# Where a rarely taken branch stands in a mixture-of-experts stage, and a PSUM bank for the last sums

## The reference, cut to what matters

```python
for g in range(N_GROUPS):
    a = jnp.einsum('td,edf->tef', t, w_gate[g])
    b = jnp.einsum('td,edf->tef', t, w_up[g])
    hid = jax.nn.silu(a) * b * comb[:, g, :, None]
    y = y + jnp.einsum('tef,efd->td', hid, w_down[g])
```

## Time and profile before

| | us |
|---|---|
| median of three runs | 1003.07 |
| the runs | 1004.33, 1001.78, 1003.07 |
| the profiled execution | 1001.91 |
| its span | 999.9 |
| TensorE busy | 946.3 (95%) |
| VectorE busy | 498.5 (50%) |
| ScalarE busy | 329.4 (33%) |

### The profile page before, as it was taken

How to read it: one execution, slowest core, us unless ns; L and a number is a source line. 1 busy time by engine, 2 the same in 40 slices (tenths; PEclk the granted TensorE clock), 3 DMA queues, 4 the chain that set the end, 5 groups by cost and what they waited for, 6 DMA issues and landing times.

```text
span 999.9 us, 14232 instructions
## 1 busy us (share of the span) xinstructions
PE 946.3 (95%) x5926; PEld 670.9 (67%) x5926; DVE 498.5 (50%) x868; ACT 329.4 (33%) x525; POOL 36.4 (4%) x39
## 2 busy tenths in 40 slices
PE   5999999999999999999898899999988899999997
PEld 5997734444444444344443689878988799999885
DVE  6694613222222222232221686988977657667642
ACT  5723210000000010000000656555464645554531
POOL 1000000000000000000000000232210000000000
PEclk9999999999999999999998999999999999999998
DMA  9946999999999999999999943623242424555301
GB/s 358 406 188 263 420 408 425 425 431 430 430 430 431 430 431 429 433 429 430 431 423 416 387 164 105 233 85 147 107 169 86 168 106 169 179 194 209 137 1 42
DMA packets 27797, 289.45 MB, mean 289 GB/s; under 512 B 3024, under 2 KB 5328, under 8 KB 11088
## 3 DMA queue, kind: packets, MB, share of 16 engines
q1 hardware_dynamic: 27008, 286.91, 70.4%
q10 hardware_dynamic: 720, 1.57, 0.4%
HBM read 287.43 MB, written 1.05 MB: 288 GB/s over the span
## 4 chain that ended last, share of the span: by engine, by line
PE 77%; DMA 9%; DVE 8%; ACT 4%; issue 2%; SPq 0%; DVEq 0%; ACTq 0%
PE ps L279 77%; DMA ring<-in_moe 8%; DVE wl L275 3%; ACT wh L268 2%; DVE arena L1497 1%; DMA vec<-in_vec 1%; PE ps L1011 1%; DVE arena L564 0%; ACT arena L1796 0%; ACT in_h L634 0%; DVE arena L1703 0%; DVE arena L1839 0%; ACT arena L1799 0%; DVE arena L365 0%; PE ps L1983 0%
## 5 line engine op out<-in xcount | busy, mean ns | idle before, releaser
L279 PE MATMUL ps<-ring,arena 128*64 128x512 f32 x1216 | 340.6, 597 | 10.2 <-issue 9.6
L279 PEld LDWEIGHTS ps<-ring,arena 128*64 128x64 f32 x1216 | 109.8, 137 | 170.0 <-issue 167.8
L275 DVE TENSOR_TENSOR wl<-ring,wh 128x1024 fp32r<-128x1024 f32 x150 | 180.7, 1234 | 58.6 <-ACT wh L268 58.6
L279 PE MATMUL ps<-arena 128*64 128x512 f32 (+3 forms) x416 | 162.9, 542 | 0.8 <-DVE arena L559 0.5
L268 ACT ACTIVATE wh<-ring 128x1024 fp32r<-128x1024 f32 x150 | 151.5, 1050 | 32.3 <-PE ps L279 28.2
L1116 DVE SCALAR_TENSOR_TENSOR arena<-ps,arena 128x512 f32<-128x512 f32 x16 | 12.0, 751 | 209.1 <-PE ps L279 209.1
L279 PE MATMUL ps<-up_h,wh 128*128 128x256 f32 x352 | 88.3, 286 | 4.6 <-DVE up_l L1920 4.6
L279 PE MATMUL ps<-up_l,wh 128*128 128x256 f32 x352 | 87.8, 284 | 0.0
L279 PEld LDWEIGHTS ps<-arena 128*64 128x64 f32 (+1 forms) x416 | 53.4, 142 | 47.0 <-issue 41.2
L1186 ACT ACTIVATE y_h<-ps 128x512 fp32r<-128x512 f32 x32 | 19.1, 597 | 158.4 <-PE ps L279 158.4
L279 PEld LDWEIGHTS ps<-up_h,wh 128*128 128x128 f32 x352 | 67.5, 192 | 5.0 <-issue 4.9
(11 more groups left out here) (262 smaller groups left out, 1505.1 us busy)
## 6 DMA issues: line engine op xcount, KB each, us to landing
ring<-in_moe SPq DMA_DIRECT2D x69, 2048.0 KB, 24.3
arena<-in_moe SPq DMA_DIRECT2D x17, 2048.0 KB, 25.5
ring<-in_w_in SPq DMA_DIRECT2D x12, 2048.0 KB, 9.4
ring<-in_w_up SPq DMA_DIRECT2D x11, 2048.0 KB, 7.9
ring<-in_moe SPq DMA_DIRECT2D x20, 512.0 KB, 15.4
ring<-in_w_dn SPq DMA_DIRECT2D x5, 2048.0 KB, 8.0
ring<-in_w_out SPq DMA_DIRECT2D x4, 2048.0 KB, 15.4
arena<-in_moe SPq DMA_DIRECT2D x12, 512.0 KB, 15.0
```

The costliest lines, as they stand in the source:

```text
L275: e.tensor_tensor(wl(i), raw_piece(i), wh(i), SUB).then_inc(*lo.up(i))
L279: return e.matmul(o, l, r, start=first, stop=final, skip_group_check=True)
```

## The change

Two edits. First, the `If` (`over`) moves from ahead of pair 15 to ahead of pair 14, on all three engines. Pair 15's place weights (`weigh(15)` on TensorE, `weighed(15)` on VectorE), which were made in pair 14, move with it, to a place just in front of it; the waits at the top of `over_dve`, which run only where the body runs, name the pair before. Second, in pair 15 the scatter of quarter 3 goes to bank 4 in place of bank 7, without the wait for the add of quarter 0.

```diff
--- before.py
+++ after.py
@@ -903,7 +903,10 @@
         scat = sig("scat", [(q, z) for q in range(NP) for z in range(4)])
         acc = sig("acc", [(q, z) for q in range(NP) for z in range(4)])
         part = sig("part", [("g", 1), ("g", 3), ("g", 5), ("u", 3)])
-        ZB = [7, 5, 6, 7]
+
+        def zb(q, z):
+
+            return 4 if (q, z) == (NP - 1, 3) else (7, 5, 6, 7)[z]
 
         def parted(q, n):
 
@@ -962,7 +965,7 @@
                     k = mm(e, ps[3][64 * r:64 * r + 64, 0:256], ident[0:NE, x:x + 1].to_broadcast([NE, CAP]), POT[0:NE, :], True,
                            True)
                 k.then_inc(*spread.up(q))
-                if q + 1 < NP:
+                if q + 1 < NP - 1:
                     if q % 2:
                         e.wait_ge(*picked.at((q + 1) // 2))
                     weigh(q + 1)
@@ -1046,12 +1049,12 @@
                 for z in (2 * n, 2 * n + 1):
                     if z == 0 and q:
                         e.wait_ge(*acc.at(q - 1, 3))
-                    if z == 3:
+                    if z == 3 and q < NP - 1:
                         e.wait_ge(*acc.at(q, 0))
                     for y in range(2):
                         f = (2 * z + y) * 128 - 512 * n
-                        mm(e, ps[ZB[z]][:, y * 256:y * 256 + 256], h[:, f:f + 128], SCT[:, :], True, False)
-                        k = mm(e, ps[ZB[z]][:, y * 256:y * 256 + 256], l[:, f:f + 128], SCT[:, :], False, True)
+                        mm(e, ps[zb(q, z)][:, y * 256:y * 256 + 256], h[:, f:f + 128], SCT[:, :], True, False)
+                        k = mm(e, ps[zb(q, z)][:, y * 256:y * 256 + 256], l[:, f:f + 128], SCT[:, :], False, True)
                     k.then_inc(*scat.up(q, z))
 
             gather(0)
@@ -1059,7 +1062,8 @@
             for q in range(NP):
                 if q == 1:
                     v = many(e)
-                elif q == NP - 1:
+                elif q == NP - 2:
+                    weigh(NP - 1)
                     over(e, v, over_pe)
                 half(q, "g")
                 if q == 0:
@@ -1127,7 +1131,7 @@
                     e.wait_ge(*scat.at(q, z))
                     if q:
                         e.wait_ge(*acc.at(q - 1, z))
-                    e.tensor_tensor(x, x, ps[ZB[z]][:, :], ADD).then_inc(*acc.up(q, z))
+                    e.tensor_tensor(x, x, ps[zb(q, z)][:, :], ADD).then_inc(*acc.up(q, z))
 
             e.wait_ge(*slots.at(0))
             pick(0)
@@ -1139,13 +1143,14 @@
             for q in range(NP):
                 if q == 1:
                     v = many(e)
-                elif q == NP - 1:
+                elif q == NP - 2:
+                    weighed(NP - 1)
                     over(e, v, over_dve)
                 hidden(q)
                 if q:
                     add(q - 1, 1)
                 placed(q)
-                if q + 1 < NP:
+                if q + 1 < NP - 1:
                     weighed(q + 1)
                 if q % 2 == 0 and q + 2 < NP:
                     pick(q // 2 + 1)
@@ -1252,8 +1257,8 @@
                     k.then_inc(*ov_d.up(x, j))
 
         def over_dve(e):
-            e.wait_ge(*ctr.at(NP - 2))
-            e.wait_ge(*acc.at(NP - 2, 1))
+            e.wait_ge(*ctr.at(NP - 3))
+            e.wait_ge(*acc.at(NP - 3, 1))
             e.wait_ge(*ppm.at(3))
             e.tensor_tensor(X1F, X1H[:, :, :], X1L[:, :, :], ADD).then_inc(*ov_in.up("sum"))
             e.wait_ge(*ov_in.at("sum"))
```

## The result

The change makes the kernel slower: 1007.13 us (median of 5 runs, 1005.48 to 1009.84) against 1003.07 (5 runs, 1001.55 to 1004.67), ratio 1.0040, 95% interval 1.0026 to 1.0053. The profiled execution took 1009.84 us, the longest of the five, with a span of 1007.9.

The account below looks back on a forecast made before the run. Weights were taken to set the pace up to 519.8 us, TensorE behind it, ScalarE the last 4 us. Part 1 at -0.1 us plus part 2 at 0 gave a median of 1003.0 us, range 999.6 to 1005.6.

Parts of the forecast that it names:

- The jump, 3.20 us: At pair 14's head: the moved check's jump costs the 3.20 us it cost ahead of pair 15.
- the jump is dearer where it is now: Rival, at pair 14's head: a second fetch or closer engine jumps add up to 3.2 us, 1006.2; chance 0.04.
- The clock: Behind the moved jump: TensorE's idleness lowers the granted clock in pair 14's gate half, costing 2.87 us.
- the 2.66 us left it high: Pair 13's idle stretch ahead of 480.56: 2.66 us of idleness did not lower TensorE's clock.
- slower: the idle stretch ahead of the gate product: Rival, 560.2 to 562.4: 2.2 us of unbroken idleness lowers the clock, +2.87 us, 1005.8; chance 0.12.
- No slack: Behind the new place: only 0.29 us of transfer wait is left to absorb the stall.
- Part 2, nothing: Pair 15's last scatter quarter in its own bank: gain 0, at most 1.25 us, since nobody is late for it.
- The other engines' jumps and the weights' new place, nothing: At pair 14: VectorE's and ScalarE's jumps add no TensorE wait; the place weights cost 0.55 us there, as before.

Follow-up runs that it names:

- move_only: Kernel before with only the check moved ahead of pair 14, pair 15's place weights in front; last quarter still in bank 7: 1006.15 us.
- weigh_late: Kernel before with pair 15's place weights moved directly in front of the check, which stays ahead of pair 15: 1004.78 us.
- weigh_early: Changed kernel with pair 15's place weights ahead of pair 13's down product, so the moved jump follows a scatter: 1003.51 us.
- bank_only: Kernel before with only the last quarter of pair 15 sent to bank 4; check stays ahead of pair 15: 1003.28 us.
- after_short: Changed kernel with the check's body cut to one expert in place of 32: 1004.73 us.
- outline_14: Changed kernel with the check's body out of line on TensorE, which falls through; ScalarE and VectorE keep their jumps: 997.77 us.
- weigh_then_fill: Changed kernel with 8 idle matmuls between the place weights and the moved jump: 1008.44 us, one run.
- after_small: Changed kernel with pair 14's up and down weights sent in quarters of their columns, so in smaller packets: 1006.58 us.
- outline_15: Kernel before with the check's body out of line on TensorE, which falls through at pair 15; other engines keep their jumps: 997.53 us.
- fill_jump: Kernel before with 20 idle matmuls directly in front of the jump ahead of pair 15: 1005.66 us.
- over_13: Kernel before with the check ahead of pair 13, the rest unmoved: 1001.83 us.

## Why the prediction was wrong

The forecast was 1003.0 us in a range of 999.6 to 1005.6; the median is 1007.13.

- **The step that failed: "The jump, 3.20 us ... I take the row, since the queue of weights is as full as it was there."** Weights and jump together took 511.79 - 506.58 = 5.21 us in place of 0.55 + 3.20 = 3.75, and 5.1 to 5.2 in move_only and weigh_late too. What raises the price is not the queue of weights, nor in the main the pair (3.62 us of idleness in weigh_early at pair 14, 3.14 in the kernel before at pair 15), but the small matmuls that the change puts directly in front of the jump. I priced weights and jump each from a row in which the other wasn't next to it, and added them. With 5.21 in the sum the forecast would have been 1004.5, inside the range. The rest of the miss, some 2.7 us, goes with the clock as far as is known: the next two points. The rival "the jump is dearer where it is now" was right in kind; it had 0.04, and a wrong cause.
- **The clock.** I took one figure, 2.87 us, for one drop. In the place where I put it, behind the moved jump, it cost 2.6 (the two halves take 16.58 us, and 13.96 at the full clock), so that term was about right, though with the whole body it varies from 1.3 (move_only, bank_only) to 2.9 (before). What the sum lacks is two other places where the clock drops in some executions and not in others. One is pair 13's wait of 2.7 us: the clock is low behind it in five profiles (after, move_only, after_short, outline_14, weigh_then_fill), and high in nine. My "the 2.66 us left it high" was one draw of it. All five have the check ahead of pair 14 (outline_14 on ScalarE and VectorE alone), as have only two of the nine (after_small, weigh_early). That is more than chance would easily give, yet nothing that the change touches runs before this wait; I have no mechanism for it, and one profile per kernel doesn't show one.
- **The rival "slower: the idle stretch ahead of the gate product" came true in the profile and was not the edit's doing.** It is the other of the two places. Without matmuls to fill the stretch, seven of eight profiles with bank 4 have the drop, and four of nine with bank 7 (move_only, outline_15, fill_jump, over_13), where the idleness is in two pieces of 1.25 and 0.73 us. So 2.2 us without a break aren't needed for it. It may come more often with the one long stretch, but bank_only's median moved by 0.2 us. Its price was 1.5 us in the product, against the 2.87 I gave it.
- **No slack: right.** No transfer was waited for behind the new place. The down product began 1.49 us after the turn, where I had 1.29, and pair 15's head came 8.16 us after that, where I had 8.15.
- **Part 2, nothing: right,** by bank_only, 0.9999 (0.9988 to 1.0009). The last four scatter groups run without a break and TensorE idles 2.26 us (2.2 forecast).
- **The other engines' jumps and the weights' new place, nothing: right,** by outline_14 against outline_15.

What remains: the profiles give 2.7 us for the weights in front of the jump; move_only's median is 3.1 us over before and the changed kernel's 4.1, with an interval of 2.6 to 5.3. The gap goes with the clock: the changed kernel's five executions have a mean granted clock of 0.985 to 0.987, move_only's twelve 0.986 to 0.989, and at 0.987 the two take the same (1005.48 and 1005.64 us; five of 1005.22 to 1006.91). In which stretch it was low in executions without a profile, and why it is low more often in the changed kernel, is not shown.

The Trainium skill's rule in "Runtime: NRT & Kernel Launch", section "Instruction fetch mechanics", that a taken branch to a target which isn't loaded waits for a fetch, holds here: with the same computation and no branch taken on TensorE before the end of its work, 5.5 and 9.4 us are gone (outline_15, outline_14). The 108 ns of "Advanced Engine Details and Errata", section "Control Flow Timing", are no price for such a branch: 3.0 to 5.3 us of idleness were measured with the whole body, in one piece or in two.

## What to carry to other kernels

A rarely taken branch over a large body costs its fetch on the path that falls to the side of the jump, so lay the body out of line and let the common case fall through: that was worth about 5 us here, and moving the branch was worth nothing. If it must be jumped over, look at what stands directly in front of it, and don't add the prices of two neighbours read from rows where they weren't neighbours. A matrix engine that waits some 2 us on its critical path may pay again behind the wait through its clock, in some executions; work that nobody reads, put into two such waits, took 3.8 us off.

## What the runs showed of the hardware that I had not expected

- The instruction fetch of a taken branch: 2.6 to 2.8 us from the packet (0.02 MB) to the first matmul in seven profiles. With small weight packets in flight (347 of 347 under 8 KB) the idle stretch was 4.83 us, with large ones 4.80.
- TensorE's work in front of a jump does not cover the fetch: with 2.4 us of matmuls put there the idle stretch was 3.81 us, not shorter.
- Eight matmuls of 2 columns, 0.55 us in a stream, put the fetch off by 1.4 to 1.9 us.
- The same wait of 2.7 us (pair 13) leaves the clock at 2.4 GHz in nine profiles and at 1.2 GHz in five, at 1.4 to 1.7 us each. Ahead of the gate product it fell behind 2.26 us in one piece and behind 1.25 and 0.73 us in two, at 1.5 us each, and stayed high in other profiles of either kind.
